# GpSimd's queue asks for the first layer's first down weights, with a semaphore of their own, instead of SyncE's ahead of the expert loop

## What is computed

```python
def hier_moe(h, w_gr, b_gr, w_er, b_er, w_gate, w_up, w_down):
    ...
        combine = jnp.sum(jax.nn.one_hot(expert_id, N_EXPERTS, dtype=jnp.float32) * gate[..., None], axis=1)
        hg = jnp.einsum('sd,edf->sef', t, w_gate)
        hu = jnp.einsum('sd,edf->sef', t, w_up)
        act = jax.nn.silu(hg) * hu * combine[:, :, None].astype(t.dtype)
        return jnp.einsum('sef,efd->sd', act, w_down)
...
    for i in range(DEPTH):
        mod = cs @ w_mod[i] + b_mod[i]
        ...
        x = x + g_f[:, None, :] * hier_moe(h, ...)
    return rmsnorm(x, norm_out)
```

## Time and profile before

| | |
|---|---|
| median of 3 runs | 732.12 us (731.3 to 732.17) |
| the profiled execution | 731.96 us |
| its span in the trace | 729.5 us |
| mean granted clock of TensorE | 0.987 |
| busy: PE, PEld, DVE, ACT, POOL | 641.2, 386.8, 372.6, 174.0, 24.9 us |
| HBM read | 268.16 MB, 369 GB/s over the span |
| queue q1 (hardware_dynamic: SyncE's) | 268.22 MB, 90.6% of 16 DMA engines |
| queue q0 (software_dynamic: GpSimd's) | 1.00 MB, 0.7% |

### The profile page before, as it was taken

One profiled execution on the slowest core, in us unless ns is written; L12 is line 12 of the kernel. 1 busy time (PEld: TensorE's weight loads), 2 busy tenths in 40 slices (PEclk: granted clock), 3 DMA queues, 4 the chain that ended last, 5 costly groups with the idle time before them and its releaser, 6 DMA issues.

```text
span 729.5 us, 11410 instructions
## 1 busy us (share of the span) xinstructions
PE 641.2 (88%) x4226; PEld 386.8 (53%) x4226; DVE 372.6 (51%) x902; ACT 174.0 (24%) x370; POOL 24.9 (3%) x54
## 2 busy tenths in 40 slices
PE   2699998999998889988899888999898899888994
PEld 1487565466654545445554445775445455455542
DVE  1268868967644533443334477664344334433345
ACT  2113441033411211122112240342113111221113
POOL 5100400000000000000000000000000000000000
PEclk9999999999999999999999999799999999999998
DMA  8999535997699999999999999887999999999991
GB/s 335 351 398 398 174 116 192 410 360 281 256 421 421 421 421 423 422 421 423 422 422 422 417 399 409 338 339 306 423 422 420 420 422 422 422 421 423 422 392 58
DMA packets 49677, 269.61 MB, mean 370 GB/s; under 512 B 3796, under 2 KB 5908, under 8 KB 25072
## 3 DMA queue, kind: packets, MB, share of 16 engines
q1 hardware_dynamic: 48864, 268.22, 90.6%
q0 software_dynamic: 784, 1.00, 0.7%
HBM read 268.16 MB, written 1.05 MB: 369 GB/s over the span
## 4 chain that ended last, share of the span: by engine, by line
PE 48%; DMA 38%; SPq 5%; DVE 5%; issue 2%; ACT 1%; POOL 0%; DVEq 0%; POOLq 0%; ACTq 0%
DMA ring<-in_w_up 35%; PE bank L875 9%; PE bank L854 8%; PE bank L889 5%; PE bank L592 4%; PE bank L739 4%; DMA early_w<-in_w_in 3%; PE bank L804 2%; PE bank L522 2%; PE bank L664 2%; PE bank L674 2%; PE bank L759 1%; PE bank L842 1%; SPq L346 1%; PE bank L627 1%
## 5 line engine op out<-in xcount | busy, mean ns | idle before, releaser
L854 PE MATMUL bank<-ring,arena 128*64 128x256 f32 x1024 | 117.3, 382 | 28.9 <-DMA ring<-in_w_up 28.8
L842 PE MATMUL bank<-ring,arena 128*64 128x256 f32 x1024 | 117.6, 382 | 12.8 <-DMA ring<-in_w_gate 12.8
L1139 ACT CAST xn_parts<-arena 128x512 fp32r<-128x512 f32 x64 | 39.6, 619 | 305.6 <-DVE arena L1591 305.6
L854 PEld LDWEIGHTS bank<-ring,arena 128*64 128x64 f32 x1024 | 71.1, 137 | 74.3 <-DMA ring<-in_w_up 41.2
L875 PE MATMUL bank<-dn_w,hT 128*64 128x512 f32 x480 | 109.5, 598 | 0.7 <-DMA dn_w<-in_w_down 0.7
L842 PEld LDWEIGHTS bank<-ring,arena 128*64 128x64 f32 x1024 | 81.1, 137 | 41.9 <-issue 16.8
L1566 DVE SCALAR_TENSOR_TENSOR hT<-hT,bank 128x256 f32<-128x256 f32 x32 | 19.8, 619 | 118.1 <-PE bank L854 118.1
L889 PE MATMUL bank<-xn_parts,sel 128*128 128x512 f32 x256 | 67.1, 406 | 0.0
L875 PEld LDWEIGHTS bank<-dn_w,hT 128*64 128x64 f32 x480 | 32.0, 136 | 62.4 <-issue 61.0
L1591 DVE SCALAR_TENSOR_TENSOR arena<-bank,hT,gates 128x512 f32<-128x512 f32 x64 | 48.0, 749 | 23.5 <-PE bank L875 23.5
L889 PEld LDWEIGHTS bank<-xn_parts,sel 128*128 128x128 f32 x256 | 45.8, 188 | 20.9 <-issue 12.4
(11 more groups left out here) (282 smaller groups left out, 676.1 us busy)
## 6 DMA issues: line engine op xcount, KB each, us to landing
ring<-in_w_gate SPq DMA_DIRECT2D x32, 2048.0 KB, 13.7
ring<-in_w_up SPq DMA_DIRECT2D x32, 2048.0 KB, 18.2
dn_w<-in_w_down SPq DMA_DIRECT2D x30, 2048.0 KB, 10.3
ring<-in_w_mod SPq DMA_DIRECT2D x23, 2048.0 KB, 16.5
ring<-in_w_in SPq DMA_DIRECT2D x2, 2048.0 KB, 21.1
ring<-in_w_down SPq DMA_DIRECT2D x2, 2048.0 KB, 14.6
early_w<-in_w_in SPq DMA_DIRECT2D x1, 2048.0 KB, 21.0
dn_w<-in_w_in SPq DMA_DIRECT2D x1, 2048.0 KB, 17.2
```

The lines of the kernel that those rows point to most:

```text
L842: ins = pe.matmul(bank[2][h * WIN:(h + 1) * WIN, 0:FE], xw[:, b, h, k, :], w[:, h, 0, k, :], start=(k == 0), stop=(k == KT - 1))
L854: ins = pe.matmul(bank[3][h * WIN:(h + 1) * WIN, 0:FE], xw[:, b, h, k, :], w[:, h, 1, k, :], start=(k == 0), stop=(k == KT - 1))
L1139: act.copy(xn_parts[:, 0, b, at], y_s[:, b, at]).then_inc(e["y_hi"], 1)
```

## The change

- In the first layer SyncE no longer waits for `dve_used` and no longer asks for down(0). It goes on to wait for `win_ready` and into the loop. The second layer is as before.
- GpSimd waits for `dve_used` to reach 8 behind `power(1)`, and asks for the same 2 MB, with the new semaphore `dn_first`.
- TensorE waits for `dn_first` ahead of down(0) of the first layer. As `dn_in[0]` now counts one load less, the later waits of that layer are for 16 less.
- ScalarE's last instruction raises `x_scaled` instead of `out_act`, which is gone, and SyncE's first output transfer waits for 3 on it. VectorE has raised it twice by then, as ScalarE itself waits for.

```diff
@@ SyncE
                 gate_load(l, 1, 2)
                 up_load(l, 1, 2)
-                if l == 0:
-                    sp.wait_ge(S["dve_used"], by_dve.index(m5b) + 1)
-                else:
+                if l == 1:
                     sp.wait_ge(S["mix_done"], 10)
-                down(l, 0)
+                    down(l, 0)
                 sp.wait_ge(S["win_ready"], l + 1)
@@
-                sp.wait_ge(S["out_dve" if t else "out_act"], 1)
+                sp.wait_ge(*((S["x_scaled"], 3), (S["out_dve"], 1))[t])
@@ GpSimd
             power(1)
+            pool.wait_ge(S["dve_used"], by_dve.index(m5b) + 1)
+            pool.dma_start(dn_w[:, :].rearrange("p o t d -> p o (t d)"),
+                           w_down[0][0:2].rearrange("o (p t) d -> p o (t d)", t=FT)).then_inc(S["dn_first"], 16)
             power(2)
@@ TensorE
                         if n >= 1:
-                            pe.wait_ge(dn_in[l], p * 16)
+                            if l == 0 and n == 1:
+                                pe.wait_ge(S["dn_first"], 16)
+                            else:
+                                pe.wait_ge(dn_in[l], (p - 1) * 16 if l == 0 else p * 16)
                             down(p - 1, dn_w)
@@ ScalarE
-            act.activation(xn[:, 0, :], xn[:, 0, :], ACT.Identity, scale=stat[:, 4:5]).then_inc(S["out_act"], 1)
+            act.activation(xn[:, 0, :], xn[:, 0, :], ACT.Identity, scale=stat[:, 4:5]).then_inc(S["x_scaled"], 1)
```

More of the change, by code:

```diff
@@ L266, in trunk @@
             slot_ready sel_ready rows_turned rows_act rows_dve xg_done xg_act xg_dve xw_half win_ready
-            row_done row_kept pool_ready x_scaled out_act out_dve out_stored dve_own pool_own""".split()
+            row_done row_kept pool_ready x_scaled out_dve out_stored dn_first dve_own pool_own""".split()
         S = {n: sem(n) for n in names}
```

## The result

The changed kernel is slower. In the first comparison it took 738.12 us in the median (737.2 to 738.78) against 731.94, a ratio of 1.0063 with an interval of 1.0036 to 1.0091; in a second one 737.49 us against 732.83, 1.0051 with an interval of 1.0028 to 1.0074. By these ratios that is 3.7 to 4.6 us, where 2.7 was forecast; the medians themselves lie 6.2 and 4.7 us apart, and both stand above 736.6 us, the top of the range that was given. The profiled execution took 737.2 us with a span of 734.8 us, 5.3 more than before.

The account below looks back on a forecast made before the run. Loads bound the expert loops (DMA at 422 GB/s). Down(0), sharing the engines, lands at 207.9: L - 205.2 = +2.7 us, carried to the end; 731.96 + 2.7 = 734.7, on the median 734.8 us, range 730.8 to 736.6.

Parts of the forecast that it names:

- The time: Whole kernel: 734.8 us on the median, +2.7 us, with 734.1 to 735.3 from the ends of down(0)'s landing; chance 0.65.
- two queues cost more than they carry: Rival: all traffic falls when GpSimd's queue sets in, down(0) lands at 209.0 to 209.7 us; +3.8 to +4.5, 736.3 us; chance 0.08.
- The bound and the place: First layer's expert loop: DMA-bound; idle DMA hole from 188.5 to 194.5 us not all to be had; shift carried to end.
- The times of issue: Gate(2) issued at 190.55 us, up(2) about 193.95, down(0) 193.9; t = 0 is the end of VectorE's sum, then 193.79.
- When GpSimd's queue begins to flow: GpSimd's down(0) load in the first layer: bytes flow 2.2 to 4.1 us after issue, between 196.1 and 198.0 us.
- The share: DMA engines during down(0): queues take turns, GpSimd's getting close to half the bytes (43% seen earlier), so 4.97 us takes 9.94.
- one-piece rival: DMA engines finish GpSimd's part of down(0) without turns; it lands at 202.3 to 204.2 us; -1.3 us, 730.8; chance 0.17.
- The landing: Down(0)'s semaphore in the first layer: between 207.2 and 208.4 us, taken as 207.9.
- What that costs: TensorE's down(0) starts at 207.9 instead of 203.89 us; next loads issued 3.8 later; step 5's up matmuls shift +2.7 us.
- L: Landing time of down(0) in the first layer; step 5's up matmuls start at L + 3.8 + 48.7, a difference of L - 205.2.
- The rest is nothing: GpSimd's later work, TensorE's new wait constant, the output semaphore exchange and the second layer: no cost.

## Why the prediction was right, and by how much it was short

- *The time.* The direction was right and the size too small: both medians, 738.12 and 737.49 us, lie above the forecast of 734.8 and above the range's upper end of 736.6, which belonged to a rival, "two queues cost more than they carry". Its price of 3.8 to 4.5 us is near the measured 4.8 by luck: the traffic did not fall when GpSimd's queue set in (427 GB/s from 203 to 205.84 us), and what was missing lay elsewhere.
- *The bound and the place.* Right. The loop is bound by its loads, the hole ahead of it could not be had, and the shift of step 5 was carried to the end.
- *The times of issue.* Right: t - 3.1, t + 0.2 and t + 0.3.
- *When GpSimd's queue begins to flow.* I had 2.2 to 4.1 us after its issue. In the changed kernel its first packets fell between 199.5 and 200 us, 3.6 to 4.1 after the issue at 195.85, at the late end. This lateness cost nothing against one queue: down(0) would have had to stand behind gate(2) until then.
- *The share.* I had close to a half; it was 51%. The one-piece rival fell with this. By the Trainium skill, "DMA: Bandwidth & Descriptors", section "SWDGE vs HWDGE vs iDMA", a DMA engine changes over between packets, and these are preferably of up to 4096 B, so that a row of 8 KB would be a packet of its own. The traces agree, with 211 packets for 1.73 MB, 8.2 KB each, and with turns of one row.
- *The landing.* I took t + 14.1 and gave up to t + 14.6; it was t + 14.6 to 14.7 in three traces. 0.5 to 0.6 us short of what I took.
- *What that costs.* Here the step failed that read "down(1), gate(3) and up(3) are issued 3.8 us after that start, as before". That was measured on a TensorE that had not idled. After 4.4 us without work its clock was at half, and down(0) took 5.3 to 6.2 us instead of 3.6: a term of +1.7 to +2.6 us that the sum did not have. The sum with it, for the first trace: L at t + 14.67 instead of 14.11 (+0.6), +1.7 for the clock, and -0.2 since the restart (from the issue of down(1) to the up matmuls of step 5) took 48.5 us instead of 48.7, make 2.7 + 0.6 + 1.7 - 0.2 = 4.8, which is what was measured. The Trainium skill says it in "TensorE: Matmul & The Clock Gate", section "HAM oscillation — how this bites in real kernels": a wait for DMA that is long enough brings TensorE's clock down, and the work behind it pays. The trace agrees, and this would have had to be asked as soon as the working had arrived at a wait of 4 us.
- *The rest is nothing.* Nothing measured speaks against it. The exchange of semaphores at the output was not tried by itself.

## What to carry to other kernels

A load on the critical path should not be moved to a second queue while the first has loads that are wanted later: here the DMA engines dealt evenly between the queues, row by row, so that bytes that take 5 us at full rate took 9.5. What has to go is the load that it shares with. Order within one queue does that (11.5 and 10.6 us to landing instead of 14.4), and so does holding the later load back (10.5 with two queues, 9.5 and 9.4 with one). And where a working ends in a new wait of several microseconds on TensorE, the price is the wait and what the clock then takes from the work behind it: here 4.0 to 4.4 us of waiting and 1.7 to 2.6 more, while waits of 0.4 to 1.3 us left the clock alone.

## What was not expected of the hardware

- A load of 2 MB alone in GpSimd's software queue landed in 8.1 us, nearly as soon as SyncE's in 7.5 to 7.8.
- A queue that starts while another has rows of 8 KB under way sent its first packet 3.3 to 4.1 us after its issue, GpSimd's and ScalarE's beside SyncE's and SyncE's beside GpSimd's; with the DMA engines idle SyncE's loads moved bytes from about 1.0 us on and GpSimd's from 1.4. Why is open.
- Two queues with rows of 8 KB took turns by single rows: 13 and 3 packets in one window of 0.3 us, 3 and 13 in the next.
- The first load after an idle stretch landed in anything from 7.7 to 11.6 us in three executions of one kernel, with the same neighbours, and a load behind it in the same queue inherited the difference (1.8 to 1.9 us to landing more than the first, in four traces).
